# Expert outputs added to h in PSUM accumulators instead of a trip through DRAM

## The reference

```python
logits = xf @ w_router + b_router                 # 32 experts
top_v, top_i = lax.top_k(logits, 4)               # 4 experts for each token
gates = softmax(top_v)
# for each expert e and each of its tokens
hmid = x @ w_up[e] + b_up[e]                      # 1024 -> 2048
hg = minimum(hmid[:, :1024], 7); hl = clip(hmid[:, 1024:], -7, 7)
act = hg * sigmoid(1.702 * hg) * (hl + 1)
y_e = act @ w_down[e] + b_down[e]                 # 1024 -> 1024
h = h + sum over the 4 experts of gate * y_e
y = rmsnorm(h, norm_final)
```

## Time and profile before

| | us |
|---|---|
| median of three runs | 1560.48 |
| the runs | 1559.53, 1560.48, 1568.26 |
| the profiled execution, own time | 1568.26 (the one run longer than the span) |
| its span, first to last instruction | 1565.7 |
| TensorE matmul busy | 1300.1 (83%) |
| VectorE, ScalarE, GpSimd busy | 530.9, 209.8, 225.4 |
| DMA moved | 480.52 MB, 307 GB/s over the span |

### The profile page before, as it was taken

The page is one execution under the profiler, slowest core; times in us unless marked ns, Lnnn a source line. Parts: engine busy times, 40 slices in busy tenths (PEclk is TensorE's granted clock), DMA queues, the critical chain, the costliest instruction groups (busy, mean ns, idle before and its releaser), DMA issues.

```text
span 1565.7 us, 30929 instructions
## 1 busy us (share of the span) xinstructions
PE 1300.1 (83%) x11087; PEld 697.0 (45%) x11088; DVE 530.9 (34%) x1344; ACT 209.8 (13%) x561; POOL 225.4 (14%) x349
## 2 busy tenths in 40 slices
PE   7999999999898977669998996695796886857865
PEld 5778777778786532223443332231232332312322
DVE  2999756643573251111211111111111111111155
ACT  2111232414240210000000000000000000000001
POOL 2008700124220010000100000000010000001320
PEclk9999999999999998779999997898898998978987
DMA  7586455204037789999978999999999999999996
GB/s 186 125 267 158 101 128 143 86 9 109 1 119 230 279 364 419 420 410 416 419 290 357 405 417 418 419 419 416 419 419 417 406 390 412 418 417 419 418 372 237
DMA packets 147329, 480.52 MB, mean 307 GB/s; under 512 B 15438, under 2 KB 76118, under 8 KB 114471
## 3 DMA queue, kind: packets, MB, share of 16 engines
q1 hardware_dynamic: 135695, 463.37, 77.3%
q0 software_dynamic: 2560, 10.29, 1.6%
q10 hardware_dynamic: 9024, 6.17, 1.2%
HBM read 462.42 MB, written 18.21 MB: 307 GB/s over the span
## 4 chain that ended last, share of the span: by engine, by line
PE 59%; DMA 17%; DVE 8%; issue 6%; SPq 3%; POOL 3%; ACT 2%; DVEq 1%; POOLq 0%
PE bank L1287 17%; DMA arena<-in_w_up 16%; PE bank L1299 10%; PE bank L782 9%; PE bank L1255 5%; PE bank L1273 3%; DVE acc L1826 3%; PE bank L1174 2%; PE bank L1182 2%; PE bank L865 2%; POOL acc L548 2%; SPq L447 2%; SPq L450 1%; PE bank L1082 1%; POOL temps L545 1%
## 5 line engine op out<-in xcount | busy, mean ns | idle before, releaser
L1287 PE MATMUL bank<-arena,gate 128*32 128x512 f32 x3264 | 420.0, 643 | 125.4 <-DMA arena<-in_w_up 124.8
L1287 PEld LDWEIGHTS bank<-arena,gate 128*32 128x32 f32 x3264 | 103.9, 113 | 395.8 <-issue 270.7
L782 PE MATMUL bank<-arena 128*128 128x304 f32 (+1 forms) x1024 | 263.9, 420 | 3.7 <-DMA arena<-in_w_in 2.2
L2368 DVE COPY gate<-bank 128x256 f32<-128x256 f32 x46 | 19.6, 425 | 634.9 <-PE bank L1299 634.9
L782 PEld LDWEIGHTS bank<-arena 128*128 128x128 f32 x1024 | 196.9, 193 | 68.2 <-ACT zs L1497 3.1
L1299 PE MATMUL bank<-arena,gate 128*32 128x256 f32 x3264 | 190.5, 384 | 30.9 <-ACT gate L1717 29.3
L1299 PEld LDWEIGHTS bank<-arena,gate 128*32 128x32 f32 x3264 | 112.4, 111 | 96.7 <-issue 27.1
L1826 DVE SCALAR_TENSOR_TENSOR acc<-arena,pcol,acc x240 | 126.3, 609 | 0.1
L672 POOL TENSOR_TENSOR qkv<-qkv 128x192 f32<-128x192 f32 x46 | 29.4, 639 | 613.3 <-DVE qkv L2312 613.3
L1273 PE MATMUL bank<-qkv 128*128 128x512 f32 x102 | 59.5, 666 | 49.9 <-DVE gate L2354 23.4
L1255 PE MATMUL bank<-qkv 128*32 128x256 f32 (+1 forms) x1224 | 87.2, 401 | 2.0 <-POOL qkv L675 1.2
(11 more groups left out here) (424 smaller groups left out, 1169.7 us busy)
## 6 DMA issues: line engine op xcount, KB each, us to landing
arena<-in_w_up SPq DMA_DIRECT2D x256, 1024.0 KB, 12.7
arena<-in_w_down SPq DMA_DIRECT2D x256, 512.0 KB, 8.6
arena<-in_w_in SPq DMA_DIRECT2D x32, 1024.0 KB, 10.4
y_d<-gate ACTq DMA_DIRECT2D x188, 32.0 KB, 4.9
y_d<-gate POOLq DMA_DIRECT2D x1, 4608.0 KB, 28.3
arena<-in_w_conf_out SPq DMA_DIRECT2D x4, 1024.0 KB, 5.1
arena<-in_state_dn_S SPq DMA_DIRECT2D x8, 512.0 KB, 7.3
arena<-in_w_dn_out SPq DMA_DIRECT2D x1, 4096.0 KB, 15.2
```

The costliest lines, as they stand in the source:

```text
L782: last = mm(bank[2 * (j % 2) + f][:, 0:cols.stop - cols.start], wring[:, slot, k, P * half:P * (half + 1)], rhs[:, k, cols], start=(k == 0 ...
L1287: last = mm(hidden(q)[v], xgT[:, i, SL * q0:SL * (q0 + 1)], parts(wup[k], q)[v], start=False, stop=(k == KC - 1), skip_group_check=True)
```

## The change

Tiles no longer write to DRAM. h is put into PSUM once and stays there: banks 1, 3, 5, 7 hold, for each group of 256 columns, the rows of both prompt halves; bank 6 holds the 32 sample rows, its four column groups on four groups of 32 partitions. After each tile TensorE adds its outputs there by a product with a gated one-hot matrix `pgt` of 32 slots by 288 tokens. `pgt` is made on VectorE from two rows spread over all partitions: `dest_row` (the slot of each token's four choices) and `gate_row`. The tiles' down product moves to bank 4, so that bank 6 is free. The four written-out last tiles become one (LAST = 1), the outer loop has 15 passes. The final norm reads h from PSUM.

```diff
-LAST = 4
+LAST = 1
-        y_d = nc.dram_tensor("y_d", (NE * SL + P * XPAD, D), F32, kind="Internal").ap()
+        h_bank = [bank[2 * q + 1] for q in range(G)]
+        h_last = bank[6]
+        y_bank = bank[4][:, W:2 * W]
 # GpSimd
-            pool.dma_start(y_d[NE * SL:NE * SL + P * XPAD, :]..., gate[...]).then_inc(s["y_zeroed"], 16)
-            for i in range(3):
-                choose_last(i, nx + (NE - LAST + i))
-            pool.wait_ge(s["y_stored"], nx * (16 * G) + 16 * G * (NE - LAST))
-            fetch_y(0)
-            fetch_y(1)
-            choose_last(3, nx + (NE - LAST + 3))
-            fetch_y(2)
+            choose(nx + (NE - 1))
+            selected(nx + (NE - 1))
 # TensorE
+            def add_to_h(left, right):
+                for c in range(2):
+                    for q in range(G):
+                        rows = slice(SL * q, SL * (q + 1))
+                        last = mm(h_bank[q][:, W * c:W * (c + 1)], left[rows, n_cols(c)], right[rows, :],
+                                  start=False, stop=True, skip_group_check=True)
+                for q in range(G):
+                    rows = slice(SL * q, SL * (q + 1))
+                    last = mm(h_last[rows, 0:W], left[rows, n_cols(2)], right[rows, :],
+                              start=False, stop=True, skip_group_check=True)
+                return last
+            def combine(b):
+                pe.wait_ge(s["y_ready"], b + 1)
+                pe.wait_ge(s["pg_ready"], b + 1)
+                add_to_h(pgt, ysb).then_inc(s["comb_done"], 1)
             def tile_step(b):
                 up_bias(b)
                 up(b, range(0, 4), now_in)
+                turn_act(prev)
                 gather(b + 1)
-                turn(act_h, bank[4], s["act_ready"], b, s["actt_done"])
                 down(prev, range(KC), prev_in)
                 up(b, range(4, KC), now_in)
-                turn(xg, bank[0][:, W:2 * W], s["xg_copied"], b + 2, s["xgt_done"])
+                turn_xg(b + 1)
+                combine(prev)
+            def spread_choice():      # 16 products of 128 columns, 8 of 32
+                pe.wait_ge(s["dest_ready"], 2)
+                for i, (src, banks) in enumerate(((dest, (bank[1], bank[3])), (gts, (bank[5], bank[7])))):
+                    for c in range(2):
+                        for r in range(TOPK):
+                            last = mm(banks[c][:, P * r:P * (r + 1)], src[:, c, r:r + 1].to_broadcast((P, P)), ident[:],
+                                      start=True, stop=True)
...
+            def start_h():
+                pe.wait_ge(s["spread_ready"], 5)
+                for q in range(G):
+                    last = mm(h_last[SL * q:SL * (q + 1), 0:W], ident[0:SL, 0:SL], xrow[0:SL, 2, W * q:W * (q + 1)], ...)
+                for c in range(2):
+                    for q in range(G):
+                        mm(h_bank[q][:, W * c:W * (c + 1)], ident[:], xrow[:, c, W * q:W * (q + 1)], ...)
+                pe.wait_ge(s["spread_done"], 7)
+                add_to_h(gt, bdn)
 # tile 1 ends with: turn_xg(2); spread_choice(); start_h(); combine(0)
 # turn_gates() moves from tile 16 to between tiles 0 and 1; the written-out last tiles
 # with turn_choice and combine_next go
 # ScalarE
             def tile_step(b):
+                copy_actt(b - 1)
                 copy_xg(b + 1)
-                copy_actt(b - 1)
                 sigmoid(b)
-                store_y(b - 1)
+            act.wait_ge(s["last_done"], 2)
+            for c in range(2):
+                fn(xn2[:, c, :]..., h_rows[c], ACT.Square, accum_out=fsq[:, c:c + 1]).then_inc(s["squared_last"], 1)
...
+            for q in range(G):
+                act.dma_start(a["y_sample"]...[:, W * q:W * (q + 1)], xn2[SL * q:SL * (q + 1), 2, 0:W])
 # VectorE
             def take_y(b):
                 dve.wait_ge(s["down_used"], b * KC + KC)
-                if not first(b):
-                    dve.wait_ge(s["y_stored"], b * (16 * G))
-                v.tensor_copy(ysb, bank[6][:, 0:W]).then_inc(s["y_ready"], 1)
+                v.tensor_copy(ysb, y_bank).then_inc(s["y_ready"], 1)
+            def choice(b):
+                if not first(b):
+                    dve.wait_ge(s["pg_ready"], b)
+                stt(pgtmp, dest_row, slotcol[:, bass.ds(b, 1)], gate_row, ALU.is_equal, ALU.mult).then_inc(s["chosen"], 1)
+                dve.wait_ge(s["chosen"], b * 2 + 1)
+                v.tensor_tensor(pgtmp[:, 0:2 * N2], pgtmp[:, 0:2 * N2], pgtmp[:, 2 * N2:4 * N2], ALU.add).then_inc(s["chosen"], 1)
+            def place_choice(b):
+                dve.wait_ge(s["chosen"], b * 2 + 2)
+                if not first(b):
+                    dve.wait_ge(s["comb_done"], b)
+                v.tensor_tensor(pgt, pgtmp[:, 0:N2], pgtmp[:, N2:2 * N2], ALU.add).then_inc(s["pg_ready"], 1)
             def tile_step(b):
                 take_y(b - 1)
                 match(b + 2)
+                choice(b)
                 activate(b, b + 1)
+                place_choice(b)
-            # add_tile, add_fetched, last_step: products and fetched rows added to xrow
```

More of the change, by code:

```diff
@@ L344, in build @@
         down_in = [sem(f"down_in{i}") for i in range(KC)]
-        y_in = [sem(f"y_in{i}") for i in range(3)]
         block = ctx.enter_context(nc.Block())
@@ L1407, in _ @@
[L1407 to L1413 removed]
+            b, prev = nx + (NE - 1), nx + (NE - 2)
+            now_in, prev_in = landed_for(b), landed_for(prev)
@@ new lines, in _ @@
+            up_bias(b)
+            up(b, range(0, 4), now_in)
+            turn_act(prev)
+            down(prev, range(KC), prev_in)
+            up(b, range(4, KC), now_in)
+            combine(prev)
+            turn_act(b)
+            down(b, range(KC), 16 * NE)
+            pe.wait_ge(s["y_ready"], nx + NE)
+            pe.wait_ge(s["pg_ready"], nx + NE)
+            for c in (0, 2, 1):
+                for q in range(G):
+                    rows = slice(SL * q, SL * (q + 1))
+                    into = h_last[rows, 0:W] if c == 2 else h_bank[q][:, W * c:W * (c + 1)]
+                    last = mm(into, pgt[rows, n_cols(c)], ysb[rows, :], start=False, stop=True, skip_group_check=True)
+                if c > 0:
+                    last.then_inc(s["last_done"], 1)
@@ L1416, in _ @@
+            pe.wait_ge(s["squared_last"], 1)
+            for q in range(G):
+                last = mm(bank[0][SL * q:SL * (q + 1), 0:1], isum, fsq[:, 3:4], start=True, stop=True, skip_group_check=True)
+            last.then_inc(s["last_done"], 1)
         @block.scalar
@@ L2428, in _ @@
[L2428 to L2440 removed]
+            take_y(nx + (NE - 2))
@@ new lines, in _ @@
+            choice(nx + (NE - 1))
+            activate(nx + (NE - 1), None)
+            place_choice(nx + (NE - 1))
+            take_y(nx + (NE - 1))
+            dve.wait_ge(s["last_done"], 3)
+            v.tensor_copy(fsq[:, 2:3], bank[0][:, 0:1]).then_inc(s["sums_last"], 1)
+            dve.wait_ge(s["bias_in"], 16 * 3 * G)
+            dve.wait_ge(s["router_in"], 64)
+            dve.wait_ge(s["row_rstd"], 4)
+            then(v.reciprocal(frs, frs))
+            for c in range(2):
+                stt(xn2[:, c, :].rearrange("p (q n) -> p q n", q=G), h_rows[c], frs[:, c:c + 1],
+                    nfin.rearrange("p (q n) -> p q n", q=G), ALU.mult, ALU.mult).then_inc(s["final_ready"], 1)
```

307 lines of the change are left out of this document (104 added, 203 removed).

## The result

| | kernel before | changed kernel |
|---|---|---|
| median, us (runs on the same chip) | 1564.12 (1559.53 to 1568.26, 4 runs) | 1591.43 (1589.84 to 1594.12, 4 runs) |
| span of the profiled execution | 1565.7 | 1588.8 |
| TensorE matmul busy | 1300.1 | 1385.0 |
| DMA moved | 480.52 MB | 464.98 MB |

The ratio is 1.0179, 95% interval 1.016 to 1.0199: the change made the kernel 27 us slower. The forecast was 1542, a gain of 18 us; the kernel moved the other way.

A forecast was written before the change was run, and what follows sets the result against it. The expert stage was taken as fed by DMA, TensorE nearly level. Terms 10.6 + 11.3 + 5 + 6.0 + 2 - 14.2 - 2 = 18.7 us gave 1542 us, range 1526 to 1568.

The forecast's parts named there:

- Parts 1 and 2: DMA and last tiles: y stores gone 10.6 us, twelve fetches gone 11.3, wait before the last tiles gone 5.
- The special stop before the last tiles: Between 1479 and 1485 us TensorE stops for a y store; without stores 5 us gained, bounds 2 and 6.
- The entry of the middle loop: TensorE idles 4.85 us there; turning of gates leaves it, DMA's gap of 6.0 us goes.
- Part 5: Start and tail: 2 us lost in tile 1 (0 to 6), 2 us gained at the end (0 to 4).
- Part 3: TensorE's saturated tile: 15.12 - 0.66 - 0.50 - 0.3 + 1.65 = 15.3 us period, bounds 15.2 and 17.1.
- the covers: Gather covers ScalarE's copy (0.66 us goes); new product covers VectorE's read of the up bank (0.50 goes).
- Part 4: Expert stage: two-tile experts take 32.7 us against DMA's 30.0; seven following another cost 2.7 each, net loss 14.2 us.
- The pass: Outer loop: each pass costs 2.6 us of idle in place of 0.5, so 2.1; 12 passes become 15.
- (A): Slower: TensorE takes the product's four 32x32 tiles in bank 6 one by one, period 16.5 us, 1582 us; chance 0.14.
- point of decision: Rival (A) decides from a tile period of about 15.9 us on, where the gain is gone.
- (B): No change: product at 1.95 us, passes dearer by register reads behind it, period 15.6 to 15.8, 1553 us; chance 0.30.

The follow-up runs named there:

- The experiment on the bias: Changed kernel with each tile's bias product issued before TensorE's two register reads of the landed counts: 1561.08 us, ratio 0.9977.
- that on the product's size: Changed kernel with each tile's new product cut to its first group (most expert outputs left out of h): 1536.97 us, ratio 0.9812.
- that in the kernel before: Kernel before with its bias product issued ahead of the register reads: 1565.01 us, ratio 1.0001.
- bias_first_old_turn: Changed kernel with the bias first, and the turn of the activations behind the gather again, ScalarE's copies in the old order: 1581.77 us, ratio 1.012.
- Bias first and 7 passes: Changed kernel with the bias ahead of the register reads and HEAD = 24, 7 outer passes instead of 15: 1550.50 us, ratio 0.9909.

## Why the prediction was wrong

**Parts 1 and 2, what leaves DMA: right, and a little high.** 10.6 + 11.3 + 5 = 27 us were forecast; taking stores and fetches out of the kernel before gave 23. The special stop before the last tiles is gone. The entry of the middle loop, forecast as a gain of 6.0 with an ordinary pass charged elsewhere, fell from 4.85 to 1.85 us of idle. Part 5's tail gave 2.9 us for 2; its 2 us of loss in tile 1 didn't show, the sixth issue comes 1.9 us earlier than before.

**Part 3, TensorE's period: the covers worked, and the step that failed is what they uncovered.** The 0.66 went, the 0.50 went, and the product costs 1.71 us (forecast 1.65). The sum still came out at 16.1 and not 15.3. Of the 0.8 us, 0.50 are the bare reads (0.44 of idle, and the product's last group, which is passed in 0.56 and not 0.63 us when the bias follows at once): the text let the product cover VectorE's read and asked only whether VectorE was late, not what TensorE's sequencer does in that time. The 0.50 us of wait had been the time in which it read the registers for the next tile; with the wait gone and 24 short matmuls and their weight loads in its place, the reads stood bare. The experiment on the bias removes the gap, that on the product's size shows that it needs more than the product's first group ahead of the reads, and that in the kernel before shows the reads had been hidden. Another 0.29 us are the shapes: the up half ahead of the turn takes 3.57 and not 3.46 (+0.11), each of the two turns lasts 0.37 us to the next start and not the 0.28 that the sum had booked (+0.18). The Trainium skill's rule that a change of tiling mode drains TensorE (TensorEngine Tiling (Array Packing), Key Properties) had been applied to the product alone; the turn that moved behind the up half also brings such a change, and `bias_first_old_turn` with its 3.45 agrees with the rule, at 0.1 us. With the bias first the period is 15.60, which is 15.31 and these 0.29: nothing else is missing.

**Part 4, the price of TensorE's time: the second failed step, and the larger one.** The text held that a two-tile expert behind a one-tile expert "is carried by the waiting that TensorE has there", and charged seven experts with 2.7 us. Put the measured pass into that rule: with 34.97 us in place of 32.7 the seven cost 7 x 5.0 - 4.7 = 30 us and the time would be 1558; with 36.67, as where the clock fell, 42 us and 1570. The remaining 21 to 33 us up to 1591 are the waiting that carried less than the text held. The stretches say where the view held. Between the 12th and 18th issue, where one- and two-tile experts alternate, nearly all of the added 8.3 us was carried. Between the 18th and 30th 10.0 of 44.7 us were, with 43.0 us of waiting left. Over the launch 0.63, 0.72 and 0.73 of TensorE's added time came out at the end in three pairs of kernels. A reading that fits, argued from the order of the issues and not tested by itself: with one buffer, the wait for weights in a one-tile expert is a wait for loads that TensorE had released late, so once it is behind, that wait belongs to the chain and isn't slack.

**The pass, a term of Part 4 with the wrong size.** The text took the 2.6 us of idle of one row for all twelve passes of the kernel before. They stand at six of the twelve pass ends; the others show 0.8 to 2.2 us. In the changed kernel it is 3.1 to 3.2 us at ten and 2.2 to 2.4 at five, and what the text had at nothing is the clock: the slow tiles behind seven of the passes, 1.6 to 1.7 us each. Eight passes out gave 15 us.

**The sum by measured terms.** TensorE's time grew by 0.98 us of period in 51 tiles, 50 us; by 14 us of idle at the passes and the entry (the idle time ahead of the bias beyond that of a plain tile: 62.9 - 51 x 0.48 against 49.9 - 51 x 0.50); and by 7 us of slow tiles (11.7 against 4.4): 71 us. At 0.63 to 0.73 that is 45 to 52 us. Against them stand 23 of stores and fetches and 2.9 in the tail: 19 to 26 us slower. The spans differ by 23, the medians by 27.

**The rivals.** (A) gave 1582 and had the time nearly right with the wrong mechanism: the last group takes 0.63 us at most, not 1.7, so the four tiles in one bank aren't taken one by one. The Trainium skill's caution (TensorEngine Tiling (Array Packing), Gotcha 1: PSUM Pressure), that different row tiles cannot access one PSUM bank at the same time, shows no cost in this trace. That (A) came within 9 us is luck. What (A) did have right is that added time counts in most tiles, and its point of decision, 15.9 us: at 15.6 the kernel ties with the one before (0.9977), at 16.1 it is slower. (B) named the true mechanism, "register reads for the next tile now stand behind it", and passes over 3 us, and it counted in 25 to 34 tiles, close to what was measured; but it had only 0.4 us to count. With the measured 0.8 us the same count gives 20 to 27 us for the forecast gain of 18.7, and the dearer passes come on top: (B) would have said slower.

**The best version.** Bias first and 7 passes: 1550.5 us, 0.9% below the kernel before (interval 0.7 to 1.1%) and 41 us below the changed one. The idea was sound by its DMA half; two small edits on TensorE's queue and loop brought it out.

## What to carry to other kernels

A wait in a trace can be the cover of work that the trace doesn't show, such as a sequencer's register reads: before booking it as a gain, ask what every queue does during it, and keep a long instruction between a run of short ones and the next read. A pause can also cost more than its length: look at the clock and the products behind it. Where two resources are level and one buffer ties them, measure the price of a microsecond of the one before trading it for the other (one run with a piece of work cut out gives it), since waiting seen downstream may be lateness handed on and not slack.

## What the runs showed of the hardware

- Two register reads on TensorE cost nothing behind a bias product of 1.05 us or behind eight short matmuls, and 0.44 to 0.53 us behind 24 of them (12 products of 256 columns in 1.7 us). Behind a wait on VectorE, and behind a turn of two instructions, some 0.3 to 0.7 us showed although the bias stood ahead. A loop pass with one inner step not taken showed 2.34 us of idle (at 1074.83 in the changed kernel) and one with two 3.12 to 3.16: about 0.8 us for a step that isn't taken.
- Pauses of TensorE and the clock: behind 3.1 us of idle the up half ran slow at seven of eight passes with weights at hand (5.34 us and not 3.64, granted clock 0.68 in the stretch shown), behind 1.6 and 0.5 us (bias first) at two of seven, and behind 1.9 us (product cut to its first group) at one of six. No run tested the length of the pause by itself.
- Changing the shape of the tiling cost about 0.1 us each time: 3.46 or 3.57 us for the same half of an up product, depending on what follows it.
- GpSimd's operation on 192 columns took 2.5 times as long (639 to 1616 ns) while VectorE ran operations on 1152 and 576 columns, and VectorE's own addition of 576 columns took 1.04 us beside it. With both cut to 16 columns GpSimd's was back at 635 ns and the end hadn't moved.
